# A hybrid decoder layer on one core: the mixer's last token group written out apart, and other orders of first loads, late waits, list one-hots and last tiles

## The reference

```
p  = x @ w_in + b_in                       # q k v o i f b c x
ym = sigmoid(o) * norm(mlstm_cell(q, k, v, i, f))   # 4 heads of 128, chunks of 128 tokens
yc = gate_b * conv3(gate_c * xc)           # short causal convolution
x1 = layer_norm(alpha * x + concat(ym, yc) @ w_out, ln_mix)
probs = softmax(x1 @ router_w + router_b)  # 16 experts in 4 groups
# best group by its top-2 sum, top-2 experts inside it, gates normalised
out = layer_norm(alpha * x1 + sum of gate * w_down(silu(w_gate x1) * (w_up x1)), ln_moe)
```

## Time and profile before

| what | value |
| --- | --- |
| median of 3 runs | 1715.93 us (1715.03 to 1716.71) |
| profiled execution | 1715.41 us, its span 1713.2 us |
| granted TensorE clock, mean | 0.973 of full |
| PE busy | 1615.4 us, 94% of the span |
| DVE busy | 1086.8 us, 63% |
| ACT busy | 659.3 us, 38% |
| POOL busy | 340.6 us, 20% |
| DMA queue of SP, ACT and the like (q1) | 32.8% of 16 engines |

### The profile page before, as it was taken

How to read it: one execution, slowest core, us unless ns; L and a number is a source line. 1 busy time by engine, 2 the same in 40 slices (tenths; PEclk the granted TensorE clock), 3 DMA queues, 4 the chain that set the end, 5 groups by cost and what they waited for, 6 DMA issues and landing times. The chain is left out here.

```text
span 1713.2 us, 25162 instructions
## 1 busy us (share of the span) xinstructions
PE 1615.4 (94%) x9494; PEld 1398.8 (82%) x9494; DVE 1086.8 (63%) x1799; ACT 659.3 (38%) x919; POOL 340.6 (20%) x271
## 2 busy tenths in 40 slices
PE   6999999999999999999999289999999999999993
PEld 4888888888888888888887178999999999999982
DVE  3436867557676468665586756555676667666676
ACT  2324424143332343342432324344555445544540
POOL 1100005100052001250000012222332323232332
PEclk8999999999999999999999679999999999999997
DMA  7332245332434225352223626666777777777761
GB/s 232 127 99 74 100 146 198 99 98 87 160 139 158 74 75 186 108 182 92 80 93 123 258 84 200 190 203 204 235 250 249 228 238 251 252 228 239 249 182 56
DMA packets 118922, 279.46 MB, mean 163 GB/s; under 512 B 14689, under 2 KB 16865, under 8 KB 118289
## 3 DMA queue, kind: packets, MB, share of 16 engines
q1 hardware_dynamic: 92112, 190.78, 32.8%
q0 software_dynamic: 26112, 84.95, 16.8%
q10 hardware_dynamic: 576, 2.10, 0.3%
HBM read 232.80 MB, written 48.40 MB: 164 GB/s over the span
## 5 line engine op out<-in xcount | busy, mean ns | idle before, releaser
L1054 PE MATMUL mix_acc<-mix_xT_high,mix_w_high 128*128 128x512 f32 x640 | 256.4, 401 | 7.5 <-DVE mix_w_low L791 7.5
L791 DVE TENSOR_TENSOR mix_w_low<-mix_w_raw,mix_w_high 128x2048 fp32r<-128x2048 f32 x73 | 168.5, 2309 | 144.7 <-ACT mix_w_high L646 144.4
L1056 PE MATMUL mix_acc<-mix_xT_high,mix_w_low 128*128 128x512 f32 x640 | 250.9, 392 | 0.0
L1055 PE MATMUL mix_acc<-mix_xT_low,mix_w_high 128*128 128x512 f32 x640 | 250.1, 391 | 0.0
L646 ACT ACTIVATE mix_w_high<-mix_w_raw 128x2048 fp32r<-128x2048 f32 x73 | 139.8, 1915 | 243.4 <-PE mix_acc L1056 224.2
L1789 DVE TENSOR_TENSOR moe_gate_up_low<-kept_w_gate_up_raw,moe_gate_up_high 128x2048 fp32r<-128x2048 f32 x64 | 146.6, 2291 | 80.3 <-ACT moe_gate_up_high L1661 80.3
L2117 PE MATMUL moe_gate_psum<-moe_xT_high,moe_gate_up_high 128*128 128x288 f32 x512 | 154.2, 301 | 1.4 <-DVE moe_xT_low L1806 1.4
L2119 PE MATMUL moe_up_psum<-moe_xT_high,moe_gate_up_low 128*128 128x288 f32 x512 | 152.1, 297 | 0.0
L2118 PE MATMUL moe_gate_psum<-moe_xT_low,moe_gate_up_high 128*128 128x288 f32 x512 | 151.9, 297 | 0.0
L2118 PE MATMUL moe_up_psum<-moe_xT_low,moe_gate_up_high 128*128 128x288 f32 x512 | 151.8, 296 | 0.0
L2117 PE MATMUL moe_up_psum<-moe_xT_high,moe_gate_up_high 128*128 128x288 f32 x512 | 151.6, 296 | 0.0
(11 more groups left out here) (441 smaller groups left out, 3493.2 us busy)
## 6 DMA issues: line engine op xcount, KB each, us to landing
mix_w_raw<-in_w_in SPq DMA_DIRECT2D x57, 1024.0 KB, 5.3
kept_w_gate_up_raw<-in_w_gate SPq DMA_DIRECT2D x32, 1024.0 KB
kept_w_gate_up_raw<-in_w_up SPq DMA_DIRECT2D x32, 1024.0 KB
kept_w_down_raw<-in_w_down SPq DMA_DIRECT2D x32, 1024.0 KB, 10.1
mix_w_raw<-in_w_out SPq DMA_DIRECT2D x16, 1024.0 KB, 5.0
mix_x_rows<-in_x POOLq DMA_DIRECT2D x16, 512.0 KB, 4.5
kept_conv_or_residual<-in_x POOLq DMA_DIRECT2D x16, 512.0 KB, 5.8
x<-kept_conv_or_residual POOLq DMA_DIRECT2D x12, 512.0 KB, 3.3
```

Of the source, the lines that this page charges most:

```text
L791: dve.tensor_tensor(wl[:, stage % 2], raw[:, stage % 2], wh[:, stage % 2].bitcast(F32), ALU.subtract).then_inc(split_l, 1)
L1054: pe.matmul(out, ah, bh, start=first, stop=False)
L1055: pe.matmul(out, ah, bl, start=False, stop=False)
L1056: return pe.matmul(out, al, bh, start=False, stop=last)
```

## The change

1. *Start.* The four stores of zeros leave SP's queue and go to POOL's, right behind the memset of their source. SP's wait for them moves to stage 5 of each group.
2. *Mixer.* The loops run over groups 1 and 2; group 3 is written out on every engine, with `last` (or `final`) set. It leaves out the load and split of a stage for a next group, the loads, turns and parts of a next x. In its last stage DVE does one tile after another: sum, statistics, aggregate, gain. ACT follows tile by tile. POOL adds the bias to tiles 0 to 2, and `route` adds it only to tile 3.
3. *Waits for stores.* SP and ACT leave `route` without waiting for x1 and alpha x1. In `experts` DVE waits for x1 before the one-hots, ACT for alpha x1 before the first split of down weights, and POOL for both before its first gather. The tile alpha_x1 gets another place in SBUF.
4. *List one-hots* are made in three parts, at experts 0, 1 and 2; their matmuls and `lists` move from expert 1 to 3.
5. *Tail.* PE: down(A) first, then U's column, then B in two halves (`down_end`) with the mean matmul between, into banks of their own. DVE: sums of A, then U, then B's half 0, then the quarters' mean and B's half 1; the norms of U, B, A, and those of the last list rows at the very end; one of the two row norms of batch 14 moves ahead of the last expert's first hidden block. POOL: three stores of end rows first, the three list stores last.

```diff
-            sp.wait_ge(stay_made, 1)
-            for k in range(4):
-                sp.dma_start(acc_dram[S + k * P:S + (k + 1) * P], XN[:, 0]).then_inc(zero_out, 16)
-            sp.wait_ge(zero_out, 4 * 16)
-            with sp.Fori(0, NG) as g:
+            def group(g, last):
...
                     if stage == 5:
+                        sp.wait_ge(zero_out, 4 * 16)
...
-                load_stage(g, 0, 1)
+                if not last:
+                    load_stage(g, 0, 1)
+
+            with sp.Fori(0, NG - 1) as g:
+                group(g, False)
+            group(NG - 1, True)
...
             pool.memset(XN[:, 0], 0.0).then_inc(stay_made, 1)
+            pool.wait_ge(stay_made, 1)
+            for k in range(4):
+                pool.dma_start(acc_dram[S + k * P:S + (k + 1) * P], XN[:, 0]).then_inc(zero_out, 16)
...
+            for t in range(NT - 1):
+                pool.wait_ge(ln_done, (NG - 1) * NT + t + 1)
+                pool.tensor_tensor(R[:, t], R[:, t], lnb[:], ALU.add).then_inc(v.x1_ready, 1)
...
+                    if final and stage + 1 == ST:
+                        for t in range(NT):
+                            take(g, stage, range(t, t + 1))
+                            wait_apart(dve, dve_idle, *own.due(g))
+                            dve.bn_aggr(lmv[:, t], lstat[:, t]).then_inc(lvar_done, 1)
+                            dve.wait_ge(lvar_done, g + t + 1)
+                            dve.scalar_tensor_tensor(out=R[:, t], in0=R[:, t], scalar=lmv[:, t, 0:1], in1=lng[:],
+                                                     op0=ALU.subtract, op1=ALU.mult).then_inc(ln_gained, 1)
+                        return
...
-            sp.wait_ge(x1_out, RT * 16)
...
-            act.wait_ge(ax_out, RT * 16)
...
-            row(0)
-            for t in range(1, RT):
-                row(t)
-                take(t - 1)
-            take(RT - 1)
+            row(RT - 1)
+            for t in range(RT):
+                take(t)
...
             n_rounds = trips(dve)
+            dve.wait_ge(keep.late_x1, RT * 16)
...
+                    if e == LAST:
+                        row_norm(r, LAST - 1, 0, 1)
                     hidden(r, e, 0)
...
-                    if e == 0:
-                        list_one_hots(r)
-                    row_norm(r, e - 1)
+                    if e < 3:
+                        list_one_hots(r, e)
+                    row_norm(r, e - 1, 1 if e == LAST else 0)
...
                 row_stats(r, LAST)
+                end_sums(r, A)
                 end_sums(r, U)
+                dve.wait_ge(end_half, r + 1)
+                dve.wait_ge(end_in[B], r * 16 + 16)
+                end_add(r, B, 0)
                 end_quarters(r)
-                end_norm(r, 0, U)
-                end_sums(r, A)
+                end_sums(r, B)
+                end_norm(r, 1, U)
+                end_norm(r, 2, B)
+                end_norm(r, 0, A)
                 row_norm(r, LAST)
-                end_norm(r, 1, A)
-                end_sums(r, B)
-                end_norm(r, 2, B)
...
+                        down(r, e, A)
                         down_last(r, e)
-                        down(r, e, A)
+                        pe.wait_ge(hid_done, r * (NE * FC) + NE * FC - 1)
+                        down_end(r, 0)
                         pe.wait_ge(end_sq_done, r + 1)
                         pe.matmul(px[0][:, 0:2], same[:], end_sq[:], start=True, stop=True).then_inc(end_mean, 1)
-                        down(r, e, B)
+                        down_end(r, 1)
```

More of the change, by code:

```diff
@@ L1171, in group @@
                         tile(g, stage, t)
-                        if (stage, t) in SLOT:
+                        if (stage, t) in SLOT and not (last and stage > LAST_Y):
                             extra(g, *SLOT[(stage, t)])
@@ L2001, in row_norm @@
                 dve.wait_ge(rs_done, r * len(BATCHES) + BATCHES.index(e) + 1)
-                for n, i in enumerate(BATCH[e]):
+                for n, i in list(enumerate(BATCH[e]))[first:end]:
                     rows = R[row_tile(i)]
```

233 lines of the change are left out of this document (137 added, 96 removed).

## The result

The changed kernel takes 1701.76 us (median of 4, 1701.49 to 1702.36) where the kernel before takes 1716.32 (median of 4 in the same measurement, 1715.03 to 1717.19). The ratio is 0.9915, 95% interval 0.9899 to 0.993: 14.6 us faster, clear of noise. The forecast was 1695.8 with a range of 1687.5 to 1704. The profiled execution of the changed kernel took 1701.49 us, its span is 1699.96.

A forecast was written before the change was run, and what follows sets the result against it. It took PE, busy 94% of the span, as the bound, with gains only in its waits, dropped work or the tail. -8.6 - 2.6 - 1.4 - 7.5 = -20.1 gave a median of 1695.8 us, range 1687.5 to 1704.

The forecast's parts named there:

- Part 1: First loads: earlier stage-1 load cuts PE's 7.5 wait to 0.6 and ends its half-clock stretch; -8.6 us.
- the 28.4 of the prediction: First loads: time when DVE's low part is done if the load issued at 18.75 took the same 9.7 us.
- Rival A: First loads: the zeros enter before 12 and hold stages 0 and 1 both; gain there -3, median 1701.4, chance 0.15.
- Part 2: End of the mixer: dropped turns end PE 3.7 earlier, but gains and adds hold each other; block change -1.15 us.
- the first end of part 1's range: First loads: nothing shares, the zeros take turns with the weight loads and do not delay them; -9.6 us.
- The period of 4.85: Mixer's last stage, per tile: copy and hops 1.33, POOL's add 2.42, and 1.1 for DVE's gain behind it.
- Part 3: Block change to first one-hots: x1 stores start 1.15 earlier, DVE waits only for them; 1.45 more, -2.6 in all.
- Part 4: List one-hots in three parts: PE's wait before expert 0's first down product goes; -1.4 us.
- Part 5: Tail: PE's new order, earlier DVE norms and three end-row stores issued earlier; -7.5 us.
- Rival B: End of the mixer: POOL and DVE don't hold each other, block changes 6.2 earlier; median 1689.6, chance 0.12.
- Rival C: Mixer's last group: written-out code starves for instructions, +47 there, in all +27; median 1743, chance 0.02.
- D: Tail: PE's clock stays at 1.2 GHz, 4.5 us of the delay reaching the norms; median 1700.3, chance 0.07.

The follow-up runs named there:

- e1: Changed kernel, but POOL issues the four zero stores behind its wait for the constants instead of ahead of it: 1694.46 us, ratio 0.9875.
- e2: Changed kernel, but POOL adds no bias in the last group and DVE adds all four in the route block: 1693.06 us, ratio 0.9872.
- e4: Changed kernel, but POOL's three end-row stores go last again, behind the last list store: 1705.98 us, ratio 0.9944.
- e8: Changed kernel with zero stores behind the constants, last group's bias on DVE, and x1 stored before the first down weights: 1684.74 us, ratio 0.983.
- e7: Changed kernel, but POOL instead of SP issues the store of x1 of tile 0 in the route block: 1698.95 us, one run.

## Why the prediction was right, and where it was not

The direction and the range held; the number was 6 us too low, and that has two causes, at two steps.

*Part 1, first loads: -8.6 forecast, about -3.1 measured* (7.53 to 4.85 of wait, 0.4 of slow clock). The step that failed is "SP issues that load at about 18.75" together with "if it took the same 9.7 us". Both were read from rows in which SP's queue had nothing of POOL's beside it and the load had an empty queue ahead. SP's constants go out slower when 2 MB of zeros are on the DMA engines, which delays the load by 4.3 (e1 takes 3.95 of it back), and the load, now right behind 1.5 MB of constants, takes 8.05 and not 5.3. With these two the 28.4 of the prediction becomes 35.5, which is what was measured. The forecast allowed 3.3 for what the zeros do to the low part (28.4 to 31.75), and 7.1 came; the 0.4 for a later stage 0 did not come (ACT's high part of it starts at 13.00, before at 13.1). Rival A had the size, -3, and half of the mechanism: the zeros crowd the first loads, but by holding up SP's issues, and stage 0 is not held. The prediction argued against it with the 4 GB/s of the earlier trace rows; that row ends at 16, and the 1.5 MB of constants move behind it. That rival A's 1701.4 lies next to the measured 1701.76 is luck: part 2 lost 2.3 more, and the terms below that nobody counted gave some of it back. The rule of the Trainium skill on queues that take turns ("DMA: Bandwidth & Descriptors", section "SWDGE vs HWDGE vs iDMA") spoke for the first end of part 1's range; the time came out near the other, through SP's issues, and no run here shows the turns by themselves. The stretch at the lower clock came back with the wait and cost 1.65 in place of 2.0.

*Part 2, the change of blocks: -1.15 forecast.* The 3.7 for PE's dropped turns were mis-sized: they gave 3.2. The period of 4.85 was 4.75 to 4.8 in the run, and the last copy ended 10.5 behind PE's last matmul where the forecast has 10.65. What failed is the last link, "last copy at 946.75, block changed 947.05": it took for granted that the engine that works last leaves last. POOL's DRAIN of 4.64 was in the profile of the kernel before, at 918, with 25 us between its end and the change of blocks, and it was not costed when work was moved onto POOL in front of it. It took 2.4. Without the adds, both that and the held gains go (e2), 7.7 in all.

*Part 3, -1.45 more:* right; 1.5 of it is there (1.26 and 0.24), the wait is for the x1 stores, and their landing was 0.1 off. *Part 4, -1.4:* right in place, 1.8 in size (37.27 to 35.50). *Part 5, -7.5:* 7.9 from the last wait for y rows (1634.28 before, 1628.86 after) to the end. The last norm came 30.4 after PE's last gate products, 30.7 was forecast; 3.7 are the order of POOL's issues (e4).

Not counted were 0.65 of the loop's entry at group 3, which is gone, 0.4 that the changed kernel is ahead of before 9 us, and 0.45 the other way in experts 4 to 14, whose period was 41.68 instead of 41.64; e8 has 41.63, so that is no effect of the change. Sum over the span by these: -3.1 - 0.4 - 0.65 + 1.5 - 1.5 - 1.8 + 0.45 - 7.9 = -13.4, where +1.5 is part 2: the route block began only 2.62 earlier (948.18 to 945.56) with 4.15 gained ahead of it, since the 3.2 of the turns were outweighed by the 4.8 of the held gains and the DRAIN. The measured span is 13.24 shorter.

Rival B, that the two engines do not hold each other, fell (gains of 3.02 to 3.09 beside the adds). Rival C, a last group that starves for instructions, fell: there is no wait of over 0.3 us inside it. D did not occur: the U column and both halves of B ran at full clock.

## What to carry to other kernels

Before work is moved to an engine, look at what that engine still has to do between its last instruction and the point where others wait for it, the DRAIN of a block above all; it is in the trace of before even where it costs nothing. A transfer taken off one queue and put on another still meets the first one on the DMA engines: what counts is when it runs beside the loads that PE waits for, and issuing the zeros behind the constants was worth 5.5 us here by the trace. And what a load costs is to be read from a row in which the same bytes stand ahead of it in the queue; the sizes of the transfers are in the profile, and a constant that is copied to all 128 partitions is not small (512 KB for each of the two longest here). When single executions are compared, look at the granted clock of the stretch first: it was 1.6 to 3.2 us of the difference at expert 3.

## What the runs showed of the hardware that was not expected

- POOL's DRAIN at the end of a block took 0.04 us where POOL had issued no DMA in the block, 0.12 with one landed, 1.35 with 16 landed, 4.64 with 56, but only 3.53 with 138 indirect ones. With one still under way it ended 0.1 after that one's landing (e7).
- Where the DRAIN began before the last of 56 had landed it took 9.75 (e2) and ended 2.3 after that landing at 901.5, and 8.96 (e8), again 2.3 after the last landing, so part of the 4.64 seems to pass while the landings come in. Why is open.
- With 2 MB of stores on POOL's queue single DMA issues of SP took up to 2.5 us (`mix_mh_gain`, 2.48), where the same one took 0.51 when the zeros came late (e1).
- Around the list matmuls the granted clock fell to 0.50 for 0, 3.4 or 6.8 us, with PE busy throughout, in kernels that are alike there. What decides it is open.
